# A hybrid DeltaNet layer on one core: the scan solves its 16x16 diagonal blocks on VectorE, both triangles in two alternating chains

## The reference, cut to what matters

```python
gc = jnp.cumsum(g, axis=-1)
decay = jnp.where(incl, jnp.exp(gc[..., :, None] - gc[..., None, :]), 0.0)
m = jnp.where(strict, einsum('cd,sd->cs', k * beta, k) * decay, 0.0)
a = m + eye                                    # unit triangular, inverted
attn = jnp.where(incl, einsum('cd,sd->cs', q, k) * decay, 0.0)
def step(s, inp):                              # one chunk after the other
    v_new = ui - wi @ s                        # ui, wi: solutions with a
    o = qd @ s + ai @ v_new
    s = s * exp(gl) + kd.T @ v_new
    return s, o
```

## Time and profile before

| | us |
|---|---|
| median of three runs | 3832.19 |
| lowest and highest run | 3829.12, 3832.26 |
| profiled execution: span of its records | 3830.5 |
| TensorE busy | 3625.1 (95%) |
| VectorE busy | 1860.4 (49%) |
| ScalarE busy | 1102.6 (29%) |
| GpSimd busy | 840.9 (22%) |

### The profile page before, as it was taken

How to read it: one execution, slowest core, us unless ns; L and a number is a source line. 1 busy time by engine, 2 the same in 40 slices (tenths; PEclk the granted TensorE clock), 3 DMA queues, 4 the chain that set the end, 5 groups by cost and what they waited for, 6 DMA issues and landing times. The chain is left out here.

```text
span 3830.5 us, 45733 instructions
## 1 busy us (share of the span) xinstructions
PE 3625.1 (95%) x16812; PEld 2319.9 (61%) x16812; DVE 1860.4 (49%) x2861; ACT 1102.6 (29%) x2297; POOL 840.9 (22%) x622
## 2 busy tenths in 40 slices
PE   6999997999999999779999999999978999999998
PEld 2455444888888444434444444445557887887886
DVE  4455554555566654345222322223446666666666
ACT  4266555444444521031111111112211111111113
POOL 1022222443333620020111111113321122112211
PEclk8999999999999999899999999999969999999999
DMA  7122324222221431573111131124434665565566
GB/s 286 43 84 76 99 85 130 67 82 82 82 71 61 160 99 55 176 258 126 55 55 55 55 115 55 45 72 143 146 130 155 209 210 191 205 210 195 202 210 242
DMA packets 286671, 486.28 MB, mean 127 GB/s; under 512 B 18908, under 2 KB 166911, under 8 KB 286377
## 3 DMA queue, kind: packets, MB, share of 16 engines
q1 hardware_dynamic: 263188, 425.33, 32.8%
q0 software_dynamic: 12096, 43.84, 4.4%
q10 hardware_dynamic: 11221, 14.87, 1.1%
HBM read 380.03 MB, written 103.96 MB: 126 GB/s over the span
## 5 line engine op out<-in xcount | busy, mean ns | idle before, releaser
L2660 POOL TENSOR_TENSOR mg<-mg,sg_m 128x512 f32<-128x512 f32 x64 | 98.1, 1533 | 777.7 <-DVE sg_m L2541 777.7
L3547 PE MATMUL bank<-xeT,raw_e 128*128 128x128 f32 x2304 | 267.9, 275 | 0.8 <-ACT xeT L3391 0.8
L3547 PEld LDWEIGHTS bank<-xeT,raw_e 128*128 128x128 f32 x2304 | 263.6, 192 | 8.3 <-issue 8.3
L2447 PE MATMUL bank<-hT,raw_w 128*128 128x512 f32 x576 | 261.8, 597 | 5.2 <-PEq L2251 5.2
L954 POOL TENSOR_SCALAR sg<-tmp 128x512 f32<-128x512 f32 (+1 forms) x76 | 113.4, 1493 | 428.4 <-DVE tmp L1022 368.3
L2447 PEld LDWEIGHTS bank<-hT,raw_w 128*128 128x128 f32 x576 | 110.4, 192 | 144.2 <-issue 144.2
L3547 PE MATMUL bank<-T_e,U 128*128 128x128 f32 x1536 | 176.7, 275 | 0.0
L3547 PEld LDWEIGHTS bank<-T_e,U 128*128 128x128 f32 x1536 | 174.1, 192 | 0.0
L682 PE MATMUL bank<-T_d,S_d 128*128 128x512 f32 x384 | 172.7, 596 | 0.0
L2447 PE MATMUL bank<-zT,S 128*128 128x512 f32 x384 | 172.6, 592 | 0.0
L2510 ACT ACTIVATE sg_m<-sg_m 128x512 f32<-128x512 f32 x72 | 45.4, 631 | 395.0 <-DVE sg_m L2550 395.0
(11 more groups left out here) (527 smaller groups left out, 7260.6 us busy)
## 6 DMA issues: line engine op xcount, KB each, us to landing
raw_e<-in_exp_w_gate SPq DMA_DIRECT2D x16, 3072.0 KB, 16.4
raw_e<-in_exp_w_up SPq DMA_DIRECT2D x16, 3072.0 KB, 13.0
raw_e<-in_exp_w_down SPq DMA_DIRECT2D x16, 3072.0 KB, 10.4
raw_w<-in_w_in SPq DMA_DIRECT2D x24, 1024.0 KB, 5.4
raw_d<-in_w_in SPq DMA_DIRECT2D x16, 1024.0 KB, 5.8
raw_h<-in_w_in SPq DMA_DIRECT2D x12, 1024.0 KB, 5.3
x0T<-in_ada_w SPq DMA_DIRECT2D x44, 256.0 KB, 3.0
kT<-kT_d SPq DMA_DIRECT2D x36, 256.0 KB, 2.9
```

The costliest lines, as they stand in the source:

```text
L2447: mm = pe.matmul(bank[:, :], lhs[:, k, :], rhs[:, k, :], start=first and k == 0, stop=k == 3, skip_group_check=not first)
L2660: pool.tensor_tensor(mg[:, i, :], mg[:, i, :], sg[:, i, :], ALU.add).then_inc(add_ok[i], 1)
L3547: mm = pe.matmul(bank[:, f * P:(f + 1) * P], lhs[:, k, f * P:(f + 1) * P], rhs[:, k, :], start=fresh and k == 0, stop=k == 3, skip_group_c ...
```

## The change

Six things change, all for the scan:

- `LEVELS` is [16, 32, 64]; the pair table, the identity and the pair turn are gone. A level works on four heads at once in banks 0, 1 and 2.
- The 16x16 diagonal blocks are inverted on VectorE. Nc is stored to DRAM and only its diagonal blocks are read back, one block per partition (8 blocks x 4 heads x 2 steps = 64 partitions), 256 numbers each. The solved blocks are written to a zeroed image in DRAM and read back as T. The pieces of blocks are 64 bytes long.
- The front (decays, differences, exponential, masks, Gram and attention products) runs `AHEAD` = 4 steps before the recurrence, with its own loads of keys and queries into the buffer of `raw_h`, and in bank 3 once the prologue is over.
- The loop is written out; semaphore counts are plain numbers.
- The load of `raw_h` and `gm` moves from the start of the stage to step 14.
- The projection stage's SP queue gets four DMAs that zero the image, ahead of its weight loads.

GpSimd has no share in the solving. VectorE solves the lower triangle in one chain of operations (semaphore `inv_f`) and the upper in another (`inv_b`), the two alternating. Half of the work for two steps stands at the end of an odd step, the other half in the even step after it.

```diff
-LEVELS = [2, 4, 8, 16, 32, 64]
+LEVELS = [16, 32, 64]
+BLK = 16 * P + 16
...
+    nc_d, ti_d = scr("nc_d", (STEPS, 32 * BLK)), scr("ti_d", (4, 64 * BLK))
...
                     sp.dma_start(tri[:, :, :], A["t_tri"]).then_inc(gw_in, 16)
+                    for r in range(4):
+                        sp.dma_start(ti_d[r].rearrange("(p c) -> p c", p=P), A["t_zero"]).then_inc(img_ok, 16)
...
+                    def both_blocks(b, half):
+                        x, t, u = nb[b % 2], Tb[:, b % 2, 0, :], Tb[:, b % 2, 1, :]
+                        grid = lambda v: v.rearrange("q (i c) -> q i c", c=ROWS)
+                        if half == 0:
+                            dve.wait_ge(nb_in[b % 2], 32 * (b // 2 + 1))
...
+                            link_f(dve.tensor_copy(t, unit))
+                            link_b(dve.tensor_copy(u, unit))
...
+                        for i in (range(1, HALF) if half == 0 else range(HALF, ROWS - 1)):
+                            k = ROWS - 1 - i
...
+                            dve.wait_ge(inv_f, n[0])
+                            link_f(dve.tensor_tensor(work(prod_f), x[:, i * ROWS + i + 1:(i + 1) * ROWS].unsqueeze(2).to_broadcast(low), grid(t)[:, i:i + 1, 0:i + 1].to_broadcast(low), ALU.mult))
+                            dve.wait_ge(inv_b, n[1])
+                            link_b(dve.tensor_tensor(work(prod_b), x[:, k * ROWS:k * ROWS + k].unsqueeze(2).to_broadcast(high), grid(u)[:, k:k + 1, k:ROWS].to_broadcast(high), ALU.mult))
+                            dve.wait_ge(inv_f, n[0])
+                            link_f(dve.tensor_tensor(grid(t)[:, i + 1:ROWS, 0:i + 1], grid(t)[:, i + 1:ROWS, 0:i + 1], work(prod_f), ALU.subtract))
+                            dve.wait_ge(inv_b, n[1])
+                            link_b(dve.tensor_tensor(grid(u)[:, 0:k, k:ROWS], grid(u)[:, 0:k, k:ROWS], work(prod_b), ALU.subtract))
...
+                        rest(s, 0)
+                        rest(s, 1)
+                        if s % 2 == 0 and s + 2 < STEPS:
+                            both_blocks((s + 2) // 2, 1)
+                        if merging:
+                            crossed(m, 0)
+                        if ahead:
+                            gram(f, 0)
+                        state_added(s, 0)
+                        if merging:
+                            joined(m, 0)
...
+                        if s % 2 and ahead:
+                            both_blocks((s + 3) // 2, 0)
```

VectorE's list of a step goes on, in order: the second state, the second Gram product, `crossed` of level 32, the Gram sum, `joined` of level 32, output, attention, output, `crossed` of level 64, attention, `joined` of level 64. TensorE's list of a step:

```diff
+                        key_state(s, 0)
+                        key_state(s, 1)
+                        inverse_turned(s)
+                        query_state(s, 0)
+                        query_state(s, 1)
+                        if ahead:
+                            differences(f)
+                        corrected(s, 0)
+                        corrected(s, 1)
+                        if merging:
+                            merge_inner(m, 0)
+                        if ahead:
+                            key_product(f, 0)
+                        state_update(s, 0)
+                        if merging:
+                            merge_outer(m, 0)
+                        state_update(s, 1)
+                        if ahead:
+                            key_product(f, 1)
+                        if merging:
+                            merge_inner(m, 1)
+                        output(s, 0)
+                        if merging:
+                            merge_outer(m, 1)
+                        if ahead:
+                            query_product(f, 0)
+                        output(s, 1)
+                        if merging:
+                            merge_inner(m, 2)
+                        if ahead:
+                            query_product(f, 1)
+                        if merging:
+                            merge_outer(m, 2)
```

Here `m` is `s + 1` and `f` is `s + AHEAD`; an inner part is the product L1295 and the turn L1299, an outer one the product L1305. ScalarE's list begins each step with the mixture Tq of level 16, which waits for the loaded T, and then the copies to TTF. The SP queue's list of a step, and the loads it moves the scan's own past:

```diff
+                        if s >= 1:
+                            store_output(s - 1)
+                        if s + 1 < STEPS:
+                            load_keys(s + 1)
+                            load_values(s + 1)
+                        if s % 2 and s + 2 < STEPS:
+                            load_inverse(s + 2)
+                        if s + AHEAD + 1 < STEPS:
+                            load_front(s + AHEAD + 1)
+                        if s + AHEAD < STEPS:
+                            store_gram(s + AHEAD)
+                        if s % 2 and s + AHEAD < STEPS:
+                            load_blocks((s + 3) // 2)
+                        if s % 2 == 0 and s + 2 < STEPS:
+                            store_blocks((s + 2) // 2)
+                            load_inverse(s + 2)
```

More of the change, by code:

```diff
@@ L1161, in build @@
             b4 = lambda bank: PS[bank][:, :].rearrange("p (h c) -> p h c", c=P)
[L1162 to L1164 removed]
+            mask4 = lambda m: m.unsqueeze(1).to_broadcast([P, HEADS, P])
             def mixed(v, b, h, n, first):
@@ new lines, in turned, with finished, scaled @@
+                    def turned(m, l):
+                        act.wait_ge(T_tr, level(m, l))
+                        act.activation(TTm[:, :, :].rearrange("p h c -> p (h c)"), PS[1][:, :], ACT.Copy).then_inc(TT_ok, 1)
+                    def finished(m):
+                        act.wait_ge(F_tr, m + 1)
+                        for d in range(2):
+                            act.activation(TTF[:, d].rearrange("p h c -> p (h c)"), PS[d][:, :], ACT.Copy).then_inc(fin_ok, 1)
+                    def scaled(s, d):
+                        act.wait_ge(q_mm, nth(s, d))
+                        if s >= 2:
+                            act.wait_ge(o_st[s % 2], 32 * (s // 2))
@@ L1409, in _ @@
-                    all_steps(act, step)
+                    for f in range(AHEAD):
+                        decay(f)
+                    for l in range(NL):
+                        other_halves(0, l)
+                        turned(0, l)
+                    for s in range(STEPS):
+                        f, m = s + AHEAD, s + 1
+                        if m < STEPS:
+                            other_halves(m, 0)
+                        finished(s)
+                        scaled(s, 0)
+                        scaled(s, 1)
+                        if f < STEPS:
+                            decay(f)
+                        weighted(s, 0)
+                        weighted(s, 1)
+                        if m < STEPS:
+                            turned(m, 0)
+                            for l in range(1, NL):
+                                other_halves(m, l)
+                                turned(m, l)
@@ new lines, in front @@
+                    def front(f):
+                        for d in range(2):
+                            gram(f, d)
+                        gram_sum(f)
+                        for d in range(2):
+                            attention(f, d)
+                    for f in range(AHEAD - 1):
+                        front(f)
+                    both_blocks(0, 0)
+                    both_blocks(0, 1)
+                    front(AHEAD - 1)
+                    for l in range(NL):
+                        crossed(0, l)
+                        joined(0, l)
```

643 lines of the change are left out of this document (336 added, 307 removed).

## The result

The changed kernel takes 3734.19 us (median of four runs, 3730.40 to 3740.06), the kernel before 3830.65 us beside it (3826.63 to 3832.26): a ratio of 0.975, 95% interval 0.9736 to 0.9764. It is faster, but the forecast was 3666, and the range ended at 3725. The profiled execution took 3740.06 us, its span is 3738.2.

The account below looks back on a forecast made before the run. TensorE, 95% busy, was taken as the bound: matmul work plus short waits in a serial inverse. Steps, prologue and last step end the stage 165.8 us earlier: 3830.5 - 165.8 = 3664.7, plus 1.7 gives 3666; range 3642 to 3725.

Parts of the forecast that it names:

- seven even steps: Scan steps with both solving halves on VectorE: 23.65 us each, from 22.1 plus 4.4 less 2.85 hidden.
- I take 4.4 and 3.4: VectorE's 16x16 solving per pair of steps: first half 4.4 us with its copies, second half 3.4 us.
- Half 1 is covered: Even step: VectorE's second solving half ends before level 16 needs VectorE; up to 5.2 us of it cost nothing.
- would double the element part, +1.5 and +1.3: VectorE's solving halves: if two-SBUF-input operations ran at the Gram sum's usual 1.15 us, 1.5 and 1.3 us more; not adopted.
- The cover: Even step: the second solving half hides behind other work before level 16, up to 5.2 us free.
- The link price: VectorE's solving chains: a dependent operation on n elements costs n/0.96 ns + 193, taken from the gate chain.
- rival A: The two VectorE solving chains don't overlap: halves 7.8 and 6.7 us, 46 us more, 3712 in all; chance 0.20.
- A's tail: Worst case of non-overlapping VectorE chains: beside GpSimd's work the total could reach 3734; the range left it out.
- TensorE's floor: TensorE's work per scan step, 21.9 us once levels 2, 4, 8 and the pair turn (7.1 us) go.
- Rivals B and D: Block transfers 4 us late per pair, 3700, chance 0.15; DRAM round trip sets the pair of steps, 3833, chance 0.05.
- The prologue: Before the scan's steps: first inverse ends at 699.6 instead of 678.7, 20.9 us later, range 15 to 28.
- the term for the clock: Prologue's three levels: TensorE at half clock after idling adds 2.5 us, of at most 5.3.

## Why the prediction was wrong, point by point

The sign was right and the size was not: the stage was to be 165.8 us shorter and is 94.5 (before 646.23 to 1257.5, after 644.89 to 1161.67). Outside the stage the span of the profiled execution differs by 2.2 us: the stage begins 1.3 earlier, and what follows it takes 2576.5 us instead of 2573.0. No run asks why; the four runs of the changed kernel lie 9.7 us apart. The missing 71.3 by the prediction's terms:

| term | predicted | measured | difference |
|---|---|---|---|
| stage start to first turn (the prediction's end of the inverse and 0.9) | 54.3 | 65.2 | +10.9 |
| seven odd steps | 154.7 | 154.6 | -0.1 |
| seven even steps | 165.6 | 225.6 | +60.0 |
| step 14 | 21.5 | 24.9 | +3.4 |
| steps 15 and 16 | 38.0 | 36.5 | -1.5 |
| last turn to end of stage (the last step less 0.9) | 11.4 | 10.0 | -1.4 |

- **The step that failed** is "I take 4.4 and 3.4" and with it "Half 1 is covered". The second half takes 12.5 us. The row that showed why was quoted: the earlier trace rows, the Gram sum with two SBUF inputs, 692 ns at best and 1146 in the median, with GpSimd at work beside it. I read it as a rate, "would double the element part, +1.5 and +1.3". It was a wait for one GpSimd instruction, charged per operation and not per element: a cost of 0.45 us on the 0.69 of a 512-element operation becomes 0.90 to 1.30 us instead of 0.2 on one of 60. One operation per instruction over GpSimd's ten is about 11 us, and the 18 others add 2 at 0.11 us each; the working had both numbers, 28 operations and 13.3 us of GpSimd in a step.
- **The cover** was right as such. TensorE waited 6.8 us for L1611, so 5.6 of the 12.5 cost nothing where 5.2 was given, and with GpSimd held back a half of 5.1 us left no wait at level 16. To the 6.8 exposed, 2.2 came by TensorE's clock behind the wait (the run with TensorE kept busy), and the shorter first half gave back 0.3: 23.65 + 8.7 = 32.35, measured 32.5. Without the second half the step is 23.2.
- **The first half** took 4.07 us instead of 4.4, with GpSimd idle: right. The link price and the overlap of the two chains were right; rival A (every operation drains, 7.8 and 6.7) is refuted by the spacing of 0.12 us, and by the 50 us that giving up the alternation cost.
- **The rival that came nearest** was A's tail, "beside GpSimd's work it could reach 3734": the number of the result, but by another mechanism, and the range cut it off. A price per instruction of the other engine should have been a rival by itself.
- **Odd steps, TensorE's floor, transfers** were right: 22.08 against 22.1; 2.1 and 2.2 us for transfers in 64 B pieces where 5 was the bound; the load of the inverse was 1.2 us longer than counted. Rivals B and D are refuted. The last inverse of a pair is late in odd steps as foreseen, and hidden.
- **The prologue** missed 10.9 us, mostly in the same two ways. Block 0 took 13.0 us instead of 7.8, held by six instructions of GpSimd (masks, keys, gates); the three levels took 19.6 instead of 14.6 (12.1 and 2.5 for the clock) at a clock of 0.51, so the term for the clock was too small by 5.0, and the first turn came 2.05 us behind them instead of 0.9. With GpSimd out of the way and the clock full the first turn starts at 700.0, forecast was 700.5.
- Steps 15 and 16 were counted by the level chain at 19.0 and are 18.25; step 14 has a second half too, and with that gone it is 20.98.

Step 0, at 30.9 us, is 1.6 below the other even ones. 1.15 of that is where the count begins: its turn starts 2.13 us after VectorE's first half (707.95 to 710.08) and not 0.98 (925.48 to 926.46). The rest fits TensorE's clock, one product behind the wait taking 1.10 us instead of 1.54; with TensorE kept busy step 0 is 30.35, like the others.

What stays open: which of the one-input operations pass freely beside GpSimd, and by what condition (the run with one input shows both kinds, and no run varied it).

## What to carry to other kernels

A chain of many small VectorE operations with two inputs in SBUF should not run beside GpSimd instructions that read SBUF: here each operation paid for the rest of one instruction. So count one held operation per instruction of GpSimd while it is at work, and either order GpSimd's work around the chain, cut its instructions, or take from it the piece that can't move. If a profile shows one large operation a few tenths longer beside another engine, ask whether that is a rate or a wait before scaling it down. And a wait of 6.8 us on TensorE cost more than itself: here 2.2 us a time in clock.

## What the runs showed of the hardware that was not expected

- VectorE operations with two SBUF inputs: 0.16 to 0.22 us for 15 to 64 elements with GpSimd idle (0.17 to 0.20 for 28 to 48 while it only writes), 0.90 to 1.30 beside 128x512 GpSimd instructions, 0.42 to 0.49 beside 128x128 ones. GpSimd itself was not slowed (1267 ns for R before, 1270 after).
- A 128x512 setting to zero on GpSimd (0.55 us in the mean) holds VectorE's 64x256 copy and 15-element one-input operations, 0.8 us in three, but no two-input ones.
- Alternating chains on VectorE start 0.12 us apart, each waiting for a semaphore of its own engine; dependent ones 0.24.
